# Two-layer decoder step on one core: layer 1's attention probabilities are weighted before the value product, and its handshakes are split by branch

## The reference

```python
q, kv_c, kv_s, kv_w, gts, z = split_cols(proj, ...)
o_c, p_c = cmp_attend(q, q_pos, blocks)            # means of 32-token blocks
# selected branch (for 512 tokens all 8 blocks are selected) and window branch:
p = masked_softmax(s, mask); o = einsum('bgrqs,bsgd->bqgrd', p, kv[:, :, 1])
gate = sigmoid(gts + b_gate).reshape(B, T, N_HEADS, 3)
o = gate[..., 0:1] * o_c + gate[..., 1:2] * o_s + gate[..., 2:3] * o_w
y = einsum('bte,ed->btd', o.reshape(B, T, NSA_W) * silu(z), w_out)
```

## Time and profile before

| | us |
|---|---|
| median of 3 runs (lowest, highest) | 2167.11 (2166.88, 2167.21) |
| the profiled execution | 2167.76 |
| its span, first to last instruction | 2166.0 |
| TensorE busy | 2134.1 (99%) |
| VectorE / ScalarE / GpSimd busy | 881.6 / 703.8 / 761.4 |

### The profile page before, as it was taken

How to read it: one execution, slowest core, us unless ns; L and a number is a source line. 1 busy time by engine, 2 the same in 40 slices (tenths; PEclk the granted TensorE clock), 3 DMA queues, 4 the chain that set the end, 5 groups by cost and what they waited for, 6 DMA issues and landing times. The chain is left out here.

```text
span 2166.0 us, 43620 instructions
## 1 busy us (share of the span) xinstructions
PE 2134.1 (99%) x17971; PEld 2031.3 (94%) x17971; DVE 881.6 (41%) x1831; ACT 703.8 (32%) x983; POOL 761.4 (35%) x584
## 2 busy tenths in 40 slices
PE   8999999999999999999999999999999999999998
PEld 7999999989899899999889999899898999899998
DVE  6423225135351462134356532663346532664112
ACT  5212124232242342142234322442234322444223
POOL 2444433425334344444321243214331242223441
PEclk9999999999999999999999999999999999999999
DMA  7333555637556334455534344344634345333433
GB/s 256 93 98 88 178 156 128 189 97 188 152 130 185 98 98 123 139 178 165 158 103 123 99 128 132 106 115 109 164 105 123 99 125 134 100 102 99 121 103 109
DMA packets 455224, 281.17 MB, mean 130 GB/s; under 512 B 19224, under 2 KB 445784, under 8 KB 453747
## 3 DMA queue, kind: packets, MB, share of 16 engines
q1 hardware_dynamic: 455051, 278.73, 45.8%
HBM read 249.87 MB, written 45.99 MB: 137 GB/s over the span
## 5 line engine op out<-in xcount | busy, mean ns | idle before, releaser
L345 POOL TENSOR_TENSOR w_lo<-w_raw,w_hi 128x512 fp32r<-128x512 f32 (+1 forms) x580 | 761.2, 1343 | 1371.0 <-ACT w_hi L329 1029.0
L368 PE MATMUL ps<-h_hi,w_hi 128*128 128x260 f32 x4640 | 962.8, 289 | 7.3 <-DVE h_lo L460 7.2
L368 PE MATMUL ps<-h_hi,w_lo 128*128 128x260 f32 x4640 | 934.4, 283 | 0.0
L368 PE MATMUL ps<-h_lo,w_hi 128*128 128x260 f32 x4640 | 932.8, 283 | 0.0
L368 PEld LDWEIGHTS ps<-h_hi,w_hi 128*128 128x128 f32 x4640 | 717.9, 188 | 31.5 <-issue 17.0
L368 PEld LDWEIGHTS ps<-h_hi,w_lo 128*128 128x128 f32 x4640 | 713.8, 188 | 0.0
L368 PEld LDWEIGHTS ps<-h_lo,w_hi 128*128 128x128 f32 x4640 | 712.5, 188 | 0.0
L329 ACT ACTIVATE w_hi<-w_raw 128x2048 fp32r<-128x2048 f32 x132 | 251.9, 1909 | 519.8 <-PE ps L368 497.5
L432 DVE TENSOR_TENSOR scratch<-ps,rstd 128x520 f32<-128x520 f32 x48 | 33.6, 700 | 265.9 <-PE ps L368 265.3
L469 DVE TENSOR_TENSOR xy<-ps,x_res 128x520 f32<-128x520 f32 x32 | 22.4, 700 | 256.1 <-PE ps L368 253.5
L1461 ACT ACTIVATE scratch<-ps,scratch 128x128 f32<-128x128 f32 (+3 forms) x128 | 66.3, 523 | 125.5 <-DVE scratch L1933 125.1
(11 more groups left out here) (363 smaller groups left out, 1760.6 us busy)
## 6 DMA issues: line engine op xcount, KB each, us to landing
w_raw<-in_w_in SPq DMA_DIRECT2D x113, 1024.0 KB, 5.8
w_raw<-in_w_out SPq DMA_DIRECT2D x32, 1024.0 KB, 5.9
scratch<-in_cache_kv_sel SPq DMA_DIRECT2D x256, 64.0 KB, 1.9
scratch<-in_cache_kv_win SPq DMA_DIRECT2D x128, 128.0 KB, 2.4
scratch<-in_cache_kv_cmp SPq DMA_DIRECT2D x256, 64.0 KB, 2.0
out_kvw_s<-in_cache_kv_win SPq DMA_DIRECT2D x24, 512.0 KB, 6.7
x_scratch<-xy SPq DMA_DIRECT2D x2, 4160.0 KB, 14.5
x_res<-x_scratch SPq DMA_DIRECT2D x32, 260.0 KB, 6.1
```

The lines of the kernel that those rows point to most:

```text
L345: ins = nc.gpsimd.tensor_tensor(WL[:, t.p, k:k + 4, 0:n], WR[:, t.p, k:k + 4, 0:n], WH[:, t.p, k:k + 4, 0:n].bitcast(F32), ALU.subtract)
L368: mm = nc.tensor.matmul(PS[0:m, bank + c, 0:HALF], lhsT=w[:, t.p, k, 0:m], rhs=h[:, k, c * HALF:(c + 1) * HALF], start=(k == 0 and x == 0) ...
```

## The change

The weight of each row (gate over row sum) is applied to the exponentials, in place in `pr`, before they are transposed; the value product then has features on the partitions, and both branches and the compressed branch add up in one bank for the four query tiles of a head. `back`, `combine` and `backed` go. `at_s`, `at_nm`, `at_exp` are signalled for each branch, and a new signal `at_w` stands between the weighting on DVE and the transposes on PE.

```diff
                     for r in range(2):
                         mm = M(PS[:, r, 0:(i + 1) * P], lhsT=qt[:, jj, i * P:(i + 1) * P],
                                rhs=kT[:, r, 0:(i + 1) * P], start=True, stop=True)
-                    mm.then_inc(S["at_s"], 1)
+                        mm.then_inc(S["at_s"], 1)
...
-                    pe.wait_ge(S["at_exp"], 16 * g + (n + 1))
...
                     for r in range(2):
+                        pe.wait_ge(S["at_w"], 32 * g + 2 * n + r + 1)
                         for s in range(i + 1):
                             mm = T(PS[:, 4 + r, s * P:(s + 1) * P], pr[:, 2 * (n % 2) + r, s * P:(s + 1) * P], ident)
...
-                        back(n - 1)
...
-                    if n >= 2:
-                        pe.wait_ge(S["at_be"], 16 * g + (n - 1))
-                    to = 6 + n % 2
+                    to = 6 + jj % 2
+                    if i == 0:
+                        if n == 0:
+                            pe.wait_ge(S["a_ptc"], g + 1)
+                        if jj >= 2:
+                            pe.wait_ge(S["a_yz"], 4 * g + jj - 1)
+                        M(PS[:, to, :], lhsT=S1["vzf"][:, jj], rhs=few[:, 0:TP], start=True, stop=False,
+                          skip_group_check=True)
                     for s in range(i + 1):
-                        M(PS[:, to, 0:P], lhsT=pt[:, 0, s * P:(s + 1) * P], rhs=vr[:, 0, s * P:(s + 1) * P],
-                          start=(s == 0), stop=(s == i))
+                        M(PS[:, to, i * P:(i + 1) * P], lhsT=vr[:, 0, s * P:(s + 1) * P], rhs=pt[:, 0, s * P:(s + 1) * P],
+                          start=False, stop=False, skip_group_check=True)
...
-                    M(PS[:, to, 2 * P:3 * P], lhsT=few[:, i * P:(i + 1) * P], rhs=S1["vzf"][:, jj],
-                      start=False, stop=True, skip_group_check=True).then_inc(S["at_o"], 1)
...
-                    back(15)
+                    pe.wait_ge(S["a_yz"], 4 * g + 4)
...
                     for r in range(2):
-                        ins = A(pr[:, 2 * (n % 2) + r, 0:L], PS[:, r, 0:L], ACT.Exp,
...
-                    ins.then_inc(S["at_exp"], 1); own.done("at_exp")
+                        act.wait_ge(S["at_nm"], 32 * g + 2 * n + r + 1)
+                        A(pr[:, 2 * (n % 2) + r, 0:L], PS[:, r, 0:L], ACT.Exp,
+                          bias=S1["st"][:, 4 + n % 2, r:r + 1], scale=SCALE,
+                          accum_out=S1["st"][:, n % 2, r:r + 1]).then_inc(S["at_exp"], 1); own.done("at_exp")
...
                     for r in range(2):
+                        dve.wait_ge(S["at_s"], 32 * g + 2 * n + r + 1)
                         blk = PS[:, r, i * P:(i + 1) * P]
-                        ins = TT(blk, blk, c1[:, C1_NEG:C1_NEG + P], ALU.add)
-                    step(ins)
-                    step(V.tensor_reduce(st[:, 2 + n % 2], PS[:, 0:2, 0:(i + 1) * P], AX, ALU.max))
-                    TS(st[:, 4 + n % 2], st[:, 2 + n % 2], -SCALE, None, ALU.mult).then_inc(S["at_nm"], 1)
-                    own.done("at_nm")
+                        step(TT(blk, blk, c1[:, C1_NEG:C1_NEG + P], ALU.add))
+                        top = st[:, 2 + n % 2, r:r + 1]
+                        step(V.tensor_reduce(top, PS[:, r, 0:(i + 1) * P], AX, ALU.max))
+                        TS(st[:, 4 + n % 2, r:r + 1], top, -SCALE, None, ALU.mult).then_inc(S["at_nm"], 1)
+                        own.done("at_nm")
...
+                    for r in range(2):
+                        total = st[:, n % 2, r:r + 1]
+                        dve.wait_ge(S["at_exp"], 32 * g + 2 * n + r + 1)
+                        step(V.reciprocal(total, total))
+                        p = pr[:, 2 * (n % 2) + r, 0:(i + 1) * P]
+                        TS(p, p, total, S1["gw"][:, 12 * g + 3 * jj + 1 + r, i:i + 1], ALU.mult, ALU.mult
+                           ).then_inc(S["at_w"], 1); own.done("at_w")
...
+                    dve.wait_ge(S["at_o"], 16 * g + 4 * jj + 4)
                     dve.wait_ge(S["a_z"], 4 * g + jj + 1)
-                    y = XY[:, bass.ds(4 * g + jj, 1), 0:TP]
-                    TT(y, y, XR[:, jj % 2:jj % 2 + 1, 0:TP], ALU.mult)
+                    TT(XY[:, 4 * g + jj, 0:TP], PS[:, 6 + jj % 2, :], XR[:, jj % 2, 0:TP], ALU.mult)
...
                 step(ins)
+                weight(0)
                 dve.wait_ge(S["d_eT"], g + 1)
                 CP(S1["ptc2"].rearrange("p a b -> p (a b)"), PS[:, 4, 0:128]).then_inc(S["d_ptd"], 1)
...
                     if n < 15:
                         maxima(n + 1)
-                    weight(n)
+                    if n > 0 and i == 0:
+                        gated(jj - 1)
+                    if n < 15:
+                        weight(n + 1)
...
-                        backed(n - 1)
...
-                    combine(n)
...
-                    y_lo(dve, own, 1, range(6, 10))
-                backed(15)
+                    y_lo(dve, own, 1, range(7, 10))
                 gated(3)
```

More of the change, by code:

```diff
@@ L1138, in cmp_turn @@
                     mm.then_inc(S["a_ctT"], 1)
-                def back(n, g=g):
-                    pe.wait_ge(S["at_cb"], 16 * g + (n + 1))
-                    T(PS[:, 6 + n % 2, 384:512], weighed[n % 2], ident).then_inc(S["at_bk"], 1)
                 def values(s):
@@ L1213, in _, with end_of_group @@
                         sample_rows(range(4))
[L1214 to L1216 removed]
+                    to = 6 + jj % 2
[6 more added lines that the diff above has]
+                          skip_group_check=True)
                     for s in range(i + 1):
[L1218 to L1219 removed]
+                        M(PS[:, to, i * P:(i + 1) * P], lhsT=vr[:, 0, s * P:(s + 1) * P], rhs=pt[:, 0, s * P:(s + 1) * P],
+                          start=False, stop=False, skip_group_check=True)
                     pe.wait_ge(S["at_ptb"], 16 * g + (n + 1))
                     for s in range(i + 1):
[L1222 to L1227 removed]
+                        mm = M(PS[:, to, i * P:(i + 1) * P], lhsT=vr[:, 1, s * P:(s + 1) * P],
+                               rhs=pt[:, 1, s * P:(s + 1) * P], start=False, stop=(i == 3 and s == i),
+                               skip_group_check=True)
+                    mm.then_inc(S["at_o"], 1)
                 sample_rows(range(4, 6))
[L1230 to L1232 removed]
+                def end_of_group(g=g):
+                    pe.wait_ge(S["a_yz"], 4 * g + 4)
                     pe.wait_ge(S["a_rd"], 2 * g + 2)
@@ L1940, in weight @@
-                    step(V.reciprocal(st[:, n % 2], st[:, n % 2]))
-                    step(TT(st[:, 6 + n % 2:7 + n % 2].rearrange("p o r -> p r o"),
-                            st[:, n % 2:n % 2 + 1].rearrange("p o r -> p r o"),
-                            S1["gw"][:, bass.ds(12 * g + (3 * jj + 1), 2), i:i + 1], ALU.mult))
-                def combine(n):
-                    w, ot, of = st[:, 6 + n % 2], weighed[n % 2], PS[:, 6 + n % 2]
-                    dve.wait_ge(S["at_o"], 16 * g + (n + 1))
-                    step(TS(ot, of[:, 0:P], w[:, 0:1], None, ALU.mult))
-                    step(STT(ot, of[:, P:2 * P], w[:, 1:2], ot, ALU.mult, ALU.add))
-                    TT(ot, ot, of[:, 2 * P:3 * P], ALU.add).then_inc(S["at_cb"], 1); own.done("at_cb")
@@ L1953, in backed @@
-                def backed(n):
-                    jj, i = n // 4, n % 4
-                    if g == 0 and n == 0:
+                    for r in range(2):
[5 more added lines that the diff above has]
+                           ).then_inc(S["at_w"], 1); own.done("at_w")
@@ L1957, in backed, with gated @@
+                def gated(jj):
+                    if g == 0 and jj == 0:
                         dve.wait_ge(S["x_saved"], 32)
-                    dve.wait_ge(S["at_bk"], 16 * g + (n + 1))
-                    CPR(XY[:, bass.ds(4 * g + jj, 1), i * P:(i + 1) * P], PS[:, 6 + n % 2:7 + n % 2, 384:512]
-                        ).then_inc(S["at_be"], 1); own.done("at_be")
-                def gated(jj):
+                    dve.wait_ge(S["at_o"], 16 * g + 4 * jj + 4)
                     dve.wait_ge(S["a_z"], 4 * g + jj + 1)
-                    y = XY[:, bass.ds(4 * g + jj, 1), 0:TP]
-                    TT(y, y, XR[:, jj % 2:jj % 2 + 1, 0:TP], ALU.mult)
+                    TT(XY[:, 4 * g + jj, 0:TP], PS[:, 6 + jj % 2, :], XR[:, jj % 2, 0:TP], ALU.mult)
@@ L2016, in _ @@
                         maxima(n + 1)
-                    weight(n)
+                    if n > 0 and i == 0:
+                        gated(jj - 1)
+                    if n < 15:
+                        weight(n + 1)
                     if g == 3 and n in (13, 14):
                         y_lo(dve, own, 1, range(2 * n - 26, 2 * n - 24))
-                    if n:
-                        if i == 3:
-                            t = Tile(A_BASE, 10 + jj, g, 14)
-                            dve.wait_ge(S["proj_done"], t.n + 1)
-                            dve.wait_ge(S["a_rowT"], 6 * g + 6)
```

(14 more changed lines are left out.)

11 lines of the change are left out of this document (removed).

## The result

| | before | after |
|---|---|---|
| median of 11 runs (lowest, highest), us | 2167.21 (2166.88, 2167.61) | 2172.40 (2171.58, 2173.00) |
| profiled execution, us | 2167.76 | 2172.68 |
| its span, us | 2166.0 | 2170.9 |

The changed kernel is slower by 5.2 us: ratio 1.0024, 95% interval 1.0016 to 1.0032. That is clear of the noise, and small: about 0.24%. The forecast was 2166.4 and the range ended at 2172.3. In what follows lines without a kernel's name are those of the changed kernel: transposes L1187, scores L1119, projection L367, compressed product L1213, value products L1216 and L1220, exponentials L1457; on VectorE the mask L1925, maximum L1927, negation L1928, reciprocal L1937, scaling L1939, the copy for `d_ptd` L1966, `gated` L1948 and L1949, `y_lo` L459.

A forecast was written before the change was run, and what follows sets the result against it. TensorE, busy 99%, was taken to bound the kernel. 7.3 - 5.2 - 0 - 0.6 - 0.4 - 0.6 + 0.2 = 0.7 us won; 2167.76 - 0.7 - 0.65 = 2166.4 us, range 2161.8 to 2172.3.

The forecast's parts named there:

- The savings: On TensorE: 64 `back` passes at 0.11 us go, 7.0 us, and the compressed product saves 0.3 us; 7.3 us won.
- Rival 3: On TensorE: the savings are not there, as its order could have hidden `back`; 2173.7 us, chance 0.03.
- Turn 0: Each group: the weighting ahead of the copy that signals `d_ptd` makes TensorE stand 1.3 us, 5.2 us lost in all.
- the high bound: At turn 0: GpSimd holds the first scaling until its instruction ends, 5.2 us lost; the low end was 3.4.
- Turn 1: Each group: idle time stays about as long, net 0, bounds 0.5 us a group either way.
- the tail: End of group 3: TensorE stands for `gated(3)` until about 1964.5, but waits for `h_lo` go; net 0.2 us won.
- no clock to win back: TensorE, busy 99% of the span, already runs at a granted clock of 0.999, the upper of its two levels.
- turns 4, 8 and 12: Thinnest cover, two slices: the second scaling just meets its need; 0.05 us at each of 12, 0.6 us lost, bounds 0 and 0.3 each.
- Turns 1 to 3: First head of each group: nothing net at the first of them, 0.1 us x 4 for the other two, 0.4 us lost.
- turn 14 of group 3: Its transposes wait for a copy that comes, with two `y_lo`, behind the weighting; 0.6 us lost, once.
- Rival 2: VectorE's weighting becomes the bound: two factors cost 0.2 us more than one, 7.1 us lost, 2174.2 us; chance 0.18.
- Rival 1: Smaller uncovered stall: GpSimd does not hold the two-factor scaling; 4.8 us won, 2162.3 us; chance 0.22 with its neighbours.

The follow-up runs named there:

- experiment 6: Changed kernel with GpSimd's split of one tile per group held until `d_ptd` is signalled: 2177.91 us, ratio 1.0050.
- experiment 1: Changed kernel with `gated(3)` and the sum behind it put ahead of `y_lo` 7 to 9 in group 3: 2168.71 us, ratio 1.0008.
- experiment 2: Kernel before with only the wait for `a_yz` added in `end_of_group` of group 3: 2171.73 us, ratio 1.0021.
- experiment 3: Changed kernel with z projections of heads 1 to 3 cut at 13 in place of 14: 2170.96 us, ratio 1.0017.
- experiment 4: Changed kernel with the scaling by the reciprocal alone, the gate left out, so the result differs: 2170.56 us, ratio 1.0017.
- experiment 10: Changed kernel with one `y_lo` ending turn 13, one ending turn 14, two in turn 15, `gated(3)` ahead of the last six: 2169.99 us, ratio 1.0014.
- experiment 5: Changed kernel with `y_lo` 0 and 1 of group 3 moved behind the copy of the sample rows in turn 13: 2174.26 us, ratio 1.0029.
- experiment 12: Changed kernel with ScalarE scaling turn 0, heads 1 to 3 cut at 13, and the end order of experiment 10: 2165.70 us, ratio 0.9994.
- experiment 11: Changed kernel with ScalarE scaling turn 0, cuts at 13, `y_lo` 0 and 1 behind the copy, `gated(3)` ahead of `y_lo` 4 to 9: 2170.12 us.
- experiment 7: Changed kernel with turn 0's exponentials scaled on ScalarE by factors that VectorE makes: 2170.27 us, ratio 1.0014.

## Why the prediction was wrong, step by step

**Right.** The savings, 7.3 us, from the distance between starts and not from the 272 ns of the earlier trace rows: each turn without a first product starts 0.33 earlier. Rival 3 falls with it. Turn 0: 5.2 predicted, 5.2 measured, for the reason given (experiment 6): the first scaling ends with GpSimd's instruction. There is some luck in the number, since only group 0 was read: group 3, where GpSimd ends earlier, lost 1.14 and not 1.3, and the other three a little more. The choice of the high bound, from one held row of two columns in the earlier trace rows, was the step that carried most. What the Trainium skill ("SBUF — State Buffer", Who interferes with whom) says of the engine that comes later is borne out in the main: the scaling, which reads and writes SBUF, ended 0.08 to 0.09 us behind GpSimd's instruction in groups 0 and 3. That is less than the 0.35 us that it takes alone, so the trace does not show that it did nothing at all until then. Turn 1, over its own start and that of turn 2, came out even, as said.

**Wrong: the tail, "net 0.2 us won, bounds 1.0 lost, 1.5 won".** The stand until `gated(3)` was seen and its end put at 1964.5; it ended at 1966.8, as the three `y_lo` ahead of it took 4.08 us and group 3 came 2.2 us late. That alone would have stayed inside the bounds (about 0.7 lost against the forecast). What was not in the sum is the clock: the prediction said that there was "no clock to win back", and did not ask whether one new long stand could lose it. It cost 2.6 us; with the stand split into two the same kernel takes 3.7 less (experiment 1), and the wait alone costs the kernel before 4.4 (experiment 2). The trace at hand could have raised the question: at its start the kernel before stands 9.46 us, and the products behind it start 0.43 us apart, as shown above. This is the largest missed term, and with the longer stand more than half of the error of 6.0 us (3.3).

**Mis-sized: turns 4, 8 and 12, 0.05 us each.** The walk itself was good: from the first scores to the end of the second scaling 3.77 us predicted, 3.84 measured, and "it just meets" was true of the end of the scaling. But from the end of the second scaling to the next scores it takes 0.23 us (1173.32 to 1173.55), where the one transpose between them had been put at 0.11; the time from the signal to the start behind it was in this sum nothing. With the 0.07 of the walk, most of which is the second factor, that is 0.2 in each of 12 turns, 2.3 us and not 0.6; experiments 3 and 4 take parts of it away. The bound of 0.3 each had held it. Turns 1 to 3 lost 0.7 us, not 0.4, half of it at turn 3 of group 1; I have not followed these waits one by one.

**Mis-sized: turn 14 of group 3, 0.6 us.** It was the copy L2027 behind two `y_lo`, as the prediction had it, but only the weighting was added to the chain. Later by 1.2 us, `y_lo` fell under GpSimd's three instructions and took 2.39 us, about 1 more than two free ones (1.44 in experiment 10). The loss is 1.6. Experiments 5 and 10 show that it is the place of `y_lo` that decides, and that each other place cost as much elsewhere.

Rival 2 has the right sign and in part the right mechanism, at the wrong size. Rival 1, a smaller stall, does not hold at any of its terms. All the missed terms lay on the slow side. The one at turns 4, 8 and 12 was inside its bound, turn 14 and turns 2 and 3 had been given none, and the clock was in no bound; the high end of the range, 2172.3, was put where about one of them would go wrong, not all.

**Still open**: why the clock fell in experiment 10 and not in experiment 12. Of the 4.9 us between the two profiled executions the account leaves 0.1.

## What to carry to other kernels

Where a change lets the engine that sets the time stand once for some microseconds, price the granted clock after it as well as the stand. A mean of 0.999 says nothing about it; look for a place in the trace where the engine has stood that long already, and read the distance of the starts behind it. Moving a single cheap operation ahead of a row of slow ones can win back both. Where a chain "just meets" its need at many places, put the time from a signal to the start behind it in every sum, and take the small loss, times the places, as the likely case. And test the parts of a change together and apart: the split handshakes were worth 0.6 us alone and 32 us with the weighting, so a part that looks free may be what makes the other bearable.

## What the runs showed of the hardware that was not expected

- **The clock after a stand is not fixed by the stand.** After 3.88 us, and after 6.36 us, the clock was 0.50 behind it. After stands of 2.1 and 2.8 us at turn 15 (experiments 5 and 11) it was 0.86 over 12 us. Around stands of 2.42 and 1.28 us it was 0.50 in one profile (experiment 10), and around 2.43 and 1.62 us it was 1.00 in another (12). In the first it fell while TensorE was at work: behind the stand of 2.42 us the products started 0.24 us apart for a microsecond, and 0.43 apart before the stand of 1.28 us began. The runs of experiment 10 fall into two bunches: six from 2169.17 to 2169.99 with a mean clock of 0.998 or 0.999, and five from 2170.84 to 2171.78 with 0.997; the profiled one, 2170.84, is of the second. Those of experiment 12 do the same (nine from 2165.20 to 2165.90, two at 2167.49 and 2167.82). Only one run of each was profiled, so that the bunches are the two clocks is likely and not shown; if it is so, one program, with the same order of work, sometimes pays some 2 us and sometimes not. With stands of up to 1.30 us at this place (experiment 1) and in the kernel before with 1.68 no profile shows it.
- **A second per-row factor** in a scaling costs 59 ns at 256 and at 512 columns alike (experiment 4).
- **Two columns are held as 128 are.** A product of 128x2 in SBUF took 0.48 us beside GpSimd's instruction (experiment 7) and ended at 1121.45, with the third of GpSimd's four (1121.42), like the scaling of 128x128 that took 0.85 instead of 0.35. Moving work between operations of VectorE in such a stretch moves who is held; with GpSimd held back instead, the next operations in line paid, and more.
